# Convolution sums in two PSUM banks, and a value row spread by one single-pass product

## The reference

```python
def mlstm_mixer(x, conv_buf, C0, n0, m0, w_in, b_in, conv_w, conv_b, w_q, w_k, w_v, w_out, chunk):
    proj = x @ w_in + b_in
    x_m, o_pre, i_pre, f_pre = jnp.split(
        proj, [A_INNER, 2 * A_INNER, 2 * A_INNER + A_HEADS], axis=-1)
    xp = jnp.concatenate([conv_buf.astype(x.dtype), x_m], axis=1)
    x_c = sum(xp[:, w:w + L] * conv_w[w] for w in range(A_CONV_W)) + conv_b
    x_c = jax.nn.silu(x_c)
    q = jnp.einsum('blhd,hde->blhe', xch, w_q)
    k = jnp.einsum('blhd,hde->blhe', xch, w_k) * (A_HEAD_DIM ** -0.5)
    v = jnp.einsum('blhd,hde->blhe', xmh, w_v)
...
    # one chunk of one head group
        C_new = decay[..., None, None] * C + jnp.einsum('bshd,bshe->bhde', wk, v)
```

## Time and profile before

| | |
|---|---|
| median of 3 runs | 2440.13 us |
| profiled execution | 2439.59 us |
| its span | 2437.8 us |
| PE busy | 2311.4 us, 95% of the span |
| DVE busy | 1576.5 us, 65% |
| ACT busy | 1136.2 us, 47% |
| POOL busy | 918.6 us, 38% |
| mean granted TensorE clock | 0.971 of 2.4 GHz |

### The profile page before, as it was taken

One profiled execution on the slowest core, in us unless ns is written; L12 is line 12 of the kernel. 1 busy time (PEld: TensorE's weight loads), 2 busy tenths in 40 slices (PEclk: granted clock), 3 DMA queues, 4 the chain that ended last, 5 costly groups with the idle time before them and its releaser, 6 DMA issues.

```text
span 2437.8 us, 51606 instructions
## 1 busy us (share of the span) xinstructions
PE 2311.4 (95%) x17330; PEld 2141.1 (88%) x17330; DVE 1576.5 (65%) x3494; ACT 1136.2 (47%) x2231; POOL 918.6 (38%) x754
## 2 busy tenths in 40 slices
PE   7889999989999999999999888899989999999997
PEld 6854555789999999999999877899989999999997
DVE  6404544319996999755555644189969997555555
ACT  5523333156654444455555542556544444555554
POOL 5621111077976666200000150779866662000000
PEclk9999999999999999999999988999989999999999
DMA  4487777544544444455555631545434444555552
GB/s 159 138 235 306 296 296 293 194 161 147 181 164 138 138 138 138 143 180 179 179 180 181 198 126 66 164 147 182 167 130 138 138 138 143 180 179 180 180 180 103
DMA packets 105491, 420.81 MB, mean 173 GB/s; under 512 B 12101, under 2 KB 12701, under 8 KB 95945
## 3 DMA queue, kind: packets, MB, share of 16 engines
q1 hardware_dynamic: 92728, 335.28, 40.9%
q0 software_dynamic: 12400, 83.47, 9.8%
q10 hardware_dynamic: 288, 1.08, 0.1%
HBM read 375.14 MB, written 44.63 MB: 172 GB/s over the span
## 4 chain that ended last, share of the span: by engine, by line
PE 76%; DVE 17%; issue 3%; POOL 2%; ACT 1%; DMA 1%; POOLq 0%; ACTq 0%; DVEq 0%; SPq 0%
PE pa L390 48%; PE pb L390 27%; DVE top L1220 4%; DVE top L1217 3%; POOL split L1608 2%; DVE pa L1260 1%; DVE pa L1259 1%; DVE top L1262 1%; DVE scb L1223 1%; DMA raw<-in_units 1%; DVE pb L1223 1%; DVE scb L1237 0%; DVE big L1437 0%; DVE top L1239 0%; DVE top L1256 0%
## 5 line engine op out<-in xcount | busy, mean ns | idle before, releaser
L862 ACT CAST split<-raw 128x512 fp32r<-128x512 f32 x1176 | 721.0, 619 | 928.0 <-PE pa L390 650.0
L390 PE MATMUL pa<-xh,split 128*128 128x264 f32 x5280 | 997.4, 288 | 64.1 <-DVE xl L1202 23.9
L1608 POOL TENSOR_TENSOR split<-raw,split 128x512 fp32r<-128x512 f32 x664 | 869.8, 1320 | 328.6 <-ACT split L862 306.8
L390 PEld LDWEIGHTS pa<-xh,split 128*128 128x128 f32 x5280 | 836.1, 191 | 69.6 <-POOL split L1608 30.1
L390 PE MATMUL pa<-xl,split 128*128 128x264 f32 x2640 | 755.5, 286 | 0.0
L1209 DVE TENSOR_TENSOR split<-raw,split 128x512 fp32r<-128x512 f32 x512 | 354.3, 693 | 302.3 <-ACT split L862 302.3
L390 PEld LDWEIGHTS pa<-xl,split 128*128 128x128 f32 x2640 | 506.0, 192 | 0.0
L390 PE MATMUL pa<-wsplit,split 128*128 128x264 f32 x3072 | 416.6, 285 | 6.6 <-DVE wsplit L1355 6.6
L390 PE MATMUL pb<-wsplit,split 128*128 128x264 f32 x3072 | 415.0, 284 | 0.0
L390 PEld LDWEIGHTS pa<-wsplit,split 128*128 128x128 f32 x3072 | 391.9, 189 | 6.9 <-issue 6.9
L390 PEld LDWEIGHTS pb<-wsplit,split 128*128 128x128 f32 x3072 | 390.9, 188 | 0.0
(11 more groups left out here) (238 smaller groups left out, 1655.9 us busy)
## 6 DMA issues: line engine op xcount, KB each, us to landing
raw<-in_units SPq DMA_DIRECT2D x636, 512.0 KB, 3.3
big<-in_state_in POOLq DMA_DIRECT2D x20, 1024.0 KB, 8.1
out_state_out<-big POOLq DMA_DIRECT2D x20, 1024.0 KB, 5.3
halves<-in_state_in POOLq DMA_DIRECT2D x12, 1024.0 KB, 9.0
out_state_out<-halves POOLq DMA_DIRECT2D x12, 1024.0 KB, 5.2
out_c_prompt<-big POOLq DMA_DIRECT2D x4, 1024.0 KB, 5.1
bias_rows<-scb POOLq DMA_DIRECT2D x1, 3072.0 KB, 39.3
big<-in_skeys POOLq DMA_DIRECT2D x2, 1024.0 KB, 6.8
```

The costliest lines, as they stand in the source:

```text
L390: return pe.matmul(out, lhs, rhs, start=start, stop=stop)
L862: nc.scalar.copy(split[:, 2 * (n % 2) + half, 0, :], ring[:, slot, half * 512:(half + 1) * 512]).then_inc(high_done, 1)
L1608: nc.gpsimd.tensor_tensor(split[:, v, 1, :], ring[:, (a + k) % RING, o], split_f[:, v, 0, :], ALU.subtract).then_inc(low_done["pool"], 1)
```

## The change

The two convolution sums move from SBUF to PSUM banks `pb` 2 and 3. PE's wait for `conv_done` moves ahead of the gate transposes, which write these banks.

The value rows of the samples are kept as a pair `vsplit` of 40 partitions: rows 0 to 7 hold the rounded values (ACT), rows 32 to 39 the remainder (DVE, a new subtraction at the head of each head's work), the rows between are cleared once. A selector `pick` over 40 rows takes the sample's row of both, so that one single-pass product over rounded operands adds the two. `pick` is built on the chip from the identity at the start (DVE), and the load of `sel8` goes away. `keep_v` copies the sample rows first, and PE's scores wait for the remainder too.

```diff
-    conv_acc = carve(2, XPW - 3)
+    conv_acc = pb[:, 2:4, 0:XPW - 3]
...
+    vsplit = rounded("vsplit", "big", [P, 2, DH], carve.at[0])
+    pick = rounded("pick", "scb", [P, NSM, P], carve.at[0])
...
-                          (sel4[0:HA, :, :], "sel4"), (sel8[0:NSM, :, :], "sel8")):
+                          (sel4[0:HA, :, :], "sel4")):
...
+        pe.wait_ge(sem("conv_done"), IC)
         pe.wait_ge(sem("gate_exps"), 1)
...
             pe.wait_ge(sem("v_kept"), h + 1)
+            pe.wait_ge(sem("v_low"), h + 1)
...
-            mm(pa[:, 2, :], sel8[0:NSM, b, :], vs[0:NSM, h % 2, :]).then_inc(sem("v_spread"), 1)
+            mm(pa[:, 2, :], pick[0:VROWS, b, :], vsplit[0:VROWS, h % 2, :]).then_inc(sem("v_spread"), 1)
...
-        pe.wait_ge(sem("conv_done"), IC)
         for u in range(4):
             project_qk(0, u)
...
-            for s in range(2):
-                nc.scalar.copy(vn[:, h % 2, s, :], pb[:, s, :])
-            nc.scalar.copy(vs[0:NSM, h % 2, :], pb[0:NSM, 2, :]).then_inc(sem("v_kept"), 1)
+            if h == 0:
+                act.wait_ge(sem("v_cleared"), 1)
+            nc.scalar.copy(vsplit[0:NSM, h % 2, :], pb[0:NSM, 2, :]).then_inc(sem("v_high"), 1)
+            nc.scalar.copy(vn[:, h % 2, 0, :], pb[:, 0, :])
+            nc.scalar.copy(vn[:, h % 2, 1, :], pb[:, 1, :]).then_inc(sem("v_kept"), 1)
...
+        dve.wait_ge(sem("const_in"), 16)
+        for a, b in ((0, 32), (32, VROWS)):
+            V.tensor_copy(pick[a:b], ident[a:b, a:a + NSM].rearrange("p (b o) -> p b o", o=1).to_broadcast(
+                [b - a, NSM, P]))
+        link(V.engine_nop())
+        V.tensor_copy(vsplit[0:32].rearrange("p a e -> p (a e)"), qm[0:32].rearrange("p c b k -> p (c b k)")).then_inc(
+            sem("v_cleared"), 1)
...
+            dve.wait_ge(sem("v_high"), h + 1)
+            V.tensor_tensor(vsplit[32:VROWS, h % 2, :], pb[0:NSM, 2, :], vsplit_f[0:NSM, h % 2, :],
+                            ALU.subtract).then_inc(sem("v_low"), 1)
             if h:
                 gate_sample(h - 1)
```

More of the change, by code:

```diff
@@ L121 @@
 SLOTS = 5
+VROWS = 32 + NSM
 NORMS = [("mix_g", "mix_b"), ("ffn_g", "ffn_b")] * DEPTH
@@ L201, in carve @@
             return v.rearrange("p (%s) -> p %s" % (" ".join(names), " ".join(names)), **dict(zip(names, dims)))
+        carve.at = at
         return carve
@@ L230, in _build @@
     c_out = carve(HC, DH)
+    vsplit = rounded("vsplit", "big", [P, 2, DH], carve.at[0])
+    vsplit_f = vsplit[:].bitcast(F32)
+    carve(2, DH)
     conv_out = carve(IC, 3 + 3 * NSM)
@@ L249, in _build @@
     qn = carve(HC, 4, 32)
-    conv_acc = carve(2, XPW - 3)
+    conv_acc = pb[:, 2:4, 0:XPW - 3]
     vn = carve(2, 2, DH)
-    vs = carve(2, DH)
     wk = carve(2, DH)
@@ L260, in _build @@
     sel4 = carve(HA, P)
-    sel8 = carve(NSM, P)
+    pick = rounded("pick", "scb", [P, NSM, P], carve.at[0])
+    carve(NSM, P)
     rt = carve(BIASW)
@@ L554, in _ @@
         pe.wait_ge(sem("x_in"), 16)
-        pe.wait_ge(sem("gate_in"), 80)
+        pe.wait_ge(sem("gate_in"), 64)
         for g in range(2):
@@ L992, in gates @@
         def gates():
-            act.wait_ge(sem("gate_in"), 80)
+            act.wait_ge(sem("gate_in"), 64)
             act.wait_ge(sem("gate_pre"), 1)
@@ L1706, in _constants @@
     sel4 = np.zeros((HA, HA, P), f)
-    sel8 = np.zeros((NSM, NSM, P), f)
     for i in range(HA):
         sel4[i, i] = 1
-    for i in range(NSM):
-        sel8[i, i] = 1
     onehot = np.zeros((NB, WINDOW), f)
@@ L1720, in _constants @@
     fold = (lane[:, None] % 32 == lane[None, 0:NSM]).astype(f)
-    return c, sel4, sel8, onehot, causal, fold
+    return c, sel4, onehot, causal, fold
 def kernel(x_prompt, x_sample, state_mlstm_C, state_mlstm_n, state_mlstm_m, state_mlstm_conv,
@@ L1767, in fm @@
         return np.moveaxis(a.reshape((c, P) + a.shape[1:]), 0, 1)
-    const, sel4, sel8, onehot, causal, fold = _constants()
+    const, sel4, onehot, causal, fold = _constants()
     xs = np.concatenate([A(x_prompt)[0], A(x_sample)[:, 0]], axis=0)
@@ L1781 @@
         "x": fm(xs),
-        "const": const, "cols": cols, "cols_a": cols_a, "sel4": sel4, "sel8": sel8, "onehot": onehot,
+        "const": const, "cols": cols, "cols_a": cols_a, "sel4": sel4, "onehot": onehot,
         "w_gate": w_in[:, 2 * INNER:].reshape(DC, P, 8).transpose(1, 0, 2),
```

## The result

The changed kernel takes 2407.89 us (median, 2406.03 to 2413.04) beside 2440.13 for the kernel before on the same chip: a ratio of 0.9868, 95% interval 0.9853 to 0.9883. One of the four runs of the kernel before took 2849.49 us and is left out as slow. The forecast was 2410.6. The profiled execution of the changed kernel took 2406.63 us; its span is 2404.8 us where it was 2437.8, 33.0 us less.

A forecast was written before the change was run, and what follows sets the result against it. Prediction: DVE, blocked by POOL, bounds much of the projections; PE narrowly bounds the sample steps. Gains 12.7 + 16.8 = 29.5 us from 2439.6 give 2410.1, plus 0.5 for the median; forecast range 2402 to 2418.

The forecast's parts named there:

- The convolution: Input projections: PSUM sums end DVE and POOL blocking, 2.1 us a tile; unit 18 starts at 80.2, gaining 12.7 us.
- The rule that spoke against it: Convolution tile: higher fixed cost reading PSUM and lost double rate, 0.35 us more than alone; gain 12.3 instead of 12.7.
- rows 4: Profile rows of DVE operations on PSUM, pricing a convolution operation at 0.51 us, a tile 0.15 us above alone.
- The spread: Sample steps: one single-pass product saves 0.65 us per spread; 4.0 in three heads, 4.7 in the last, together 16.8 us.
- more: Rival, chance 0.12: cheaper spread and clock kept after the projections give 2405; low clock behind each head's idle also gone, 2389.
- 32 x 0.65: Heads: every spread saving in full, 20.8 us, set aside for 16.8 because the state-update chain binds.
- Spread 0: Start of each head's sample steps: step 0 waits for DVE's first update, so only 0.39 of 0.65 us is saved.
- The preparation: Value pair and selector: new DVE remainder of about 0.7 us and selector copies hidden; costs nothing, at most 0.3 us a head.
- The stage's end moves as a whole: End of projections: POOL's loads follow its last subtraction, so PE's later wait for a unit moves with it.
- Blocking is gone: Convolution: the rival, chance 0.09, had blocking stay because rows are still read in SBUF; only 16.8 us kept, 2423.
- no step waits for a transfer: Sample steps: the rival, chance 0.11, had DMA become the bound; spreads keep 6.8 us, total gain 19.5, time 2420.
- the clock held at 1.00: Sample steps: the slower rival, chance 0.05, had PE's new small waits drop the clock to 1.2 GHz; up to 2510.

The follow-up runs named there:

- e1: The kernel before with only the convolution sums moved to PSUM (and the moved conv_done wait), spread as before: 2428.93 us, ratio 0.9951.
- after: The changed kernel itself, with both edits (convolution sums in PSUM, single-pass spread), against the kernel before: 2407.89 us, ratio 0.9868.
- e2: The changed kernel with the convolution sums back in SBUF, so only the spread is changed: 2422.95 us, ratio 0.9931.
- e5: The changed kernel with ACT's split for projection unit 18 put ahead of its last three Silus: 2407.30 us, ratio 0.9863.
- e4: The changed kernel with each spread product issued twice into the same bank: one execution, 2415.55 us.
- e7: The changed kernel with two of four groups of closing products moved between sample steps 0 and 1: 2386.86 us, ratio 0.9780.
- e6: The changed kernel with ACT's decay of the next state issued one sample step earlier: 2410.73 us, ratio 0.9879.
- e10: The changed kernel with closing products between steps 0 and 1, earlier state decay, and unit 18's split ahead of three Silus: 2384.19 us, ratio 0.9776.

## Why the prediction was right, and by how much each step

The sum of 29.5 us became 32.2 by the medians. By the traces (33.0) the convolution gave 0.8 less than forecast (11.9 of 12.7), the wait for the unit took 1.0, the heads gave 4.0 more (20.8 of 16.8), and 1.3 came from where nothing was changed. The mechanisms are in the main those forecast. The 4.0 is not from them but from the clock in one head, so that the total came out so near is in part luck.

- **The convolution: 12.7 forecast, 12.2 alone (e1).** The price of 0.51 us an operation was 0.523 and 0.521, the tile 2.10 for 2.1. The chain behind it (last sums, Silu, half a split, subtraction) left 3.48 us of idle for a forecast 3.5. Unit 18 came at 80.51 in e1 and at 81.54 in after, for 80.2. Eleven units took 32.1 us for a forecast 31.5. The 1.0 us between e1 and after is a later start: unit 7 began at 44.90 in e1 and 45.92 in after, DVE's first gate row at 26.41 and 27.42. It is not the new copies ahead of it, as e2 and e5 have them too and started at 26.84 and 26.39. e1 and after had the same end of the projections (123.9), e1 spending its lead at the low clock. One reading was loose: the long operations were 1.04 to 1.07 us over the short ones, less than the whole subtraction (1.29) that the prediction puts there.
- **The rule that spoke against it.** The Trainium skill ("VectorE: DVE Perf Modes", section "The TRN2 errata") gives a higher fixed cost for reading PSUM; by the prediction's estimate from it the tile would cost 0.35 us more than alone. Measured: 0.17 more (2.10 against 1.93), nearly all of it the multiplication's. Its smallest and middle durations went from 353 and 366 ns to 502 and 521, as they would with a double rate lost; those of the multiply-add went from 519 and 521 to 521 and 523. No extra fixed cost shows in an in-place sum, and the measurement decides for rows 4.
- **The spread: 16.8 forecast, 18.2 alone (e2).** The saving was 0.62 each for 0.65, and two steps took 10.73 us for 10.77. By head, both edits in: 8.6, 4.1, 3.7 and 4.4 us for a forecast 4.0, 4.0, 4.0 and 4.7 (which make 16.7, not 16.8). Heads two to four are near the forecast, with a little clock in them either way. The first head is where the 20.8 comes from, and it is the clock. From step 1 to the end of the closing products some 4.2 of its 8.6 us lie in products that took longer before at a lower clock: step 1 lasted 1.94 us (1.07 in after), the spread behind it 2.07 (1.12 for the other spreads of before), the closing products 9.57 (7.14 in after, at 1.00). The closing products of the first head in the kernel before, and two windows there (the clock is the third number from the end):

```profile
194.97 9.57 PE L390 MATMUL pb<-big 128*128 128x512 f32 x16
```
```profile
191.10:194.00 2.90, 2.89 (x10) 0.70 (x10) 2.83 (x3) 0.00 (x0) 1.07 (x2) 0.50 0.57 226
194.00:198.00 4.00, 4.00 (x6) 1.48 (x5) 3.97 (x6) 0.00 (x0) 0.00 (x0) 0.50 0.99 330
```

I had named this as a rival ("more"), as all or nothing for the four heads; it came in one. It is the luck of that execution as far as is known: e4, with the same stand-still, had 10.09 us there. That 20.8 is also 32 x 0.65, the sum that I had put aside, is chance.
- **Spread 0: too much, and for the wrong reason.** I had step 0 wait for DVE's first update, with 0.39 us saved of 0.65. The update ended 4.16 us behind the start of the spread, as before (170.09 to 174.25), but step 0 came only at 4.45 and did not wait for it. It came at 4.60 before, so 0.15 was saved. The rest is lost one product earlier, where PE waits 0.22 us for the weighted keys of `prompt_values` (L1497).
- **The preparation: nothing, as forecast.** DVE's subtraction took 0.68 us, and PE's wait ahead of the first head's scores stayed at 0.56.
- **The stage's end moves as a whole: nearly.** The wait for the unit was 7.96 us, 1.0 longer than before (6.96). Over the runs with the store ahead of the heads it was 6.40 to 8.56, e2 with unmoved projections among them (8.07), so the 1.0 is no more than it varies by.
- **The rivals.** Blocking is gone, no step waits for a transfer (loads land in 7.0/8.7/10.9 us), and the clock held at 1.00 from 187 to 235 us, through steps with 0.30 us waits. That is against the Trainium skill's account ("TensorE: Matmul & The Clock Gate", section "A second HAM failure mode: psum-queue depth-cycling") of another kernel, where small idles between groups swing the clock, as a rule for this one: through those waits it held; behind the 2.82 us stand-stills it mostly fell.

## What to carry to other kernels

When two engines in one loop both show tails as long as the other's instruction, look at where their operands lie before balancing their load: an in-place sum in PSUM cost 2 ns more and took the tail of up to 1.07 us off the multiply-adds. Count a short stand-still of PE with the low clock behind it, which here raised its price from 11.3 to 19.7 us, and look for independent products already in the program to fill it: two groups moved by a few lines gave 21 us, against 32 for the whole change. A wait that goes is a gain only if nothing behind it takes the time back: of the four waits taken away here, two came back at another place and one run lost its gain to a low clock.

## What the runs showed that was not expected

- The same stand-still of 2.82 us, at the same place in the same program, is followed by 1.2 GHz in some heads and not in others: in after not in the first (7.14 us for the closing products) but in the second (8.90), in e4 in the first (10.09). That is 2 to 3 us a head. It may be what spreads the runs of one kernel (e2's went from 2415.50 to 2425.75 us), which is only argued, as one execution of each was profiled. What decides it was not found.
- A low clock also came with no stand-still of that size ahead: 4.57 us for 16 products at 290.08 in after, 5.48 for the projections of step 2 in e7's first head (clock 0.72 from 186 to 192 us). That is open too. The small waits in the steps do not explain the first of these: in e6, which has none, the same products lasted 4.48 to 4.55 us in all three later heads, and in the two kernels with the old spread, before and e1, 2.88 in all of them. So the shorter spread may bring a low clock of its own, some 1.7 us each time, where the stand-still is left; in e7 and e10 it did not come. No run tested this.
